# Two down projections: a second pair of weight pieces in seven products, and products with high weights first

## The reference, cut to what matters

```python
hn = rms_norm_2(h, norm_ffn_g)
gate, up = jnp.split(hn @ w_gate_up, 2, axis=-1)      # 2048 -> 2 x 5632
h = h + (jax.nn.silu(gate) * up) @ w_down             # 5632 -> 2048
out = rms_norm_2(h, norm_final_g)
```

## Time and profile before

| what | value |
|---|---|
| median of 3 runs | 2610.51 us |
| the profiled execution | 2610.58 us |
| its span, first to last instruction | 2608.8 us |
| TensorE multiplications | 2600.0 us busy, 21492 of them |
| VectorE busy | 1679.9 us (64%) |
| ScalarE busy | 1186.8 us (45%) |
| granted clock of TensorE in the span | 1.000 |

### The profile page before, as it was taken

The page is one execution under the profiler, slowest core; times in us unless marked ns, Lnnn a source line. Parts: engine busy times, 40 slices in busy tenths (PEclk is TensorE's granted clock), DMA queues, the critical chain, the costliest instruction groups (busy, mean ns, idle before and its releaser), DMA issues.

```text
span 2608.8 us, 50524 instructions
## 1 busy us (share of the span) xinstructions
PE 2600.0 (100%) x21492; PEld 2547.7 (98%) x21492; DVE 1679.9 (64%) x1795; ACT 1186.8 (45%) x1280; POOL 14.6 (1%) x33
## 2 busy tenths in 40 slices
PE   9999999999999999999999999999999999999998
PEld 8989999999999999999999999999999989998997
DVE  7668765555555556795676666556777775567566
ACT  5356544434443444465443433444544444444444
POOL 2000000000000000000000000000000000000000
PEclk9999999999999999999999999999999999999999
DMA  9654556555655565555555555655565556555653
GB/s 307 202 168 163 196 191 197 186 201 187 198 187 200 188 199 191 178 203 197 178 194 189 184 190 182 196 191 194 194 210 194 193 194 203 193 186 196 208 189 134
DMA packets 254460, 504.29 MB, mean 193 GB/s; under 512 B 9390, under 2 KB 11712, under 8 KB 254160
## 3 DMA queue, kind: packets, MB, share of 16 engines
q1 hardware_dynamic: 250160, 496.14, 57.2%
q10 hardware_dynamic: 3136, 4.34, 0.5%
q0 software_dynamic: 992, 1.34, 0.2%
HBM read 498.89 MB, written 2.89 MB: 192 GB/s over the span
## 4 chain that ended last, share of the span: by engine, by line
PE 100%; ACT 0%; DVE 0%; DVEq 0%; POOL 0%; issue 0%; POOLq 0%
PE ps L1608 49%; PE ps L1619 25%; PE ps L1686 4%; PE ps L1695 4%; PE ps L1690 3%; PE ps L1636 3%; PE ps L1638 3%; PE ps L1637 3%; PE ps L1810 1%; PE ps L1646 1%; PE ps L1647 1%; PE ps L1809 1%; PE ps L1808 1%; PE ps L1644 1%; PE ps L1654 0%; PE ps L1561 0%
## 5 line engine op out<-in xcount | busy, mean ns | idle before, releaser
L963 DVE TENSOR_TENSOR lo<-raw,hi 128x1024 fp32r<-128x1024 f32 x939 | 1139.8, 1224 | 799.0 <-ACT hi L597 786.1
L597 ACT ACTIVATE hi<-raw 128x1024 fp32r<-128x1024 f32 x939 | 989.9, 1060 | 1206.7 <-PE ps L1619 923.4
L1608 PE MATMUL ps<-A,hi 128*128 128x256 f32 x7286 | 902.8, 276 | 0.0
L1608 PEld LDWEIGHTS ps<-A,hi 128*128 128x128 f32 x7286 | 861.0, 188 | 0.3
L1608 PE MATMUL ps<-B,hi 128*128 128x256 f32 x3963 | 491.0, 276 | 0.0
L1619 PE MATMUL ps<-A,lo 128*128 128x256 f32 x3648 | 487.7, 276 | 0.0
L1608 PEld LDWEIGHTS ps<-B,hi 128*128 128x128 f32 x3963 | 468.2, 188 | 0.1
L1619 PEld LDWEIGHTS ps<-A,lo 128*128 128x128 f32 x3648 | 447.4, 188 | 0.0
L1619 PE MATMUL ps<-B,lo 128*128 128x256 f32 x1984 | 265.2, 276 | 0.0
L1619 PEld LDWEIGHTS ps<-B,lo 128*128 128x128 f32 x1984 | 243.3, 188 | 0.0
L1686 PE MATMUL ps<-B,hi 128*128 128x260 f32 (+3 forms) x768 | 109.1, 284 | 0.0
(11 more groups left out here) (311 smaller groups left out, 1524.2 us busy)
## 6 DMA issues: line engine op xcount, KB each, us to landing
raw<-in_w_in_dram SPq DMA_DIRECT2D x135, 1024.0 KB, 5.2
raw<-in_ffn_w_dram SPq DMA_DIRECT2D x132, 1024.0 KB, 5.1
raw<-in_w_gate_up_dram SPq DMA_DIRECT2D x88, 1024.0 KB, 5.1
raw<-in_w_down_dram SPq DMA_DIRECT2D x44, 1024.0 KB, 5.1
raw<-in_w_out_dram SPq DMA_DIRECT2D x16, 1024.0 KB, 5.1
raw<-in_pl_w_gate_dram SPq DMA_DIRECT2D x16, 1024.0 KB, 5.1
raw<-in_conv_out_w_dram SPq DMA_DIRECT2D x16, 1024.0 KB, 5.0
raw<-in_w_o_dram SPq DMA_DIRECT2D x16, 1024.0 KB, 5.1
```

Of the source, the lines that this page charges most:

```text
L597: act.activation(hi[:, slot % RING], raw[:, raw_slot, 2 * (slot % 2):2 * (slot % 2) + 2, :], ACT.Copy).then_inc(hi_ready, 1)
L963: dve.tensor_tensor(lo[:, slot % RING], raw[:, slot // 2 % RAWS, 2 * (slot % 2):2 * (slot % 2) + 2, :], hi[:, slot % RING], ALU.subtract). ...
L1608: pe.matmul(ps[:, b0 + m, 0:T], high(slot, kk, m), x, start=j == 0 and kk == 0 and part == 0, stop=False)
```

## The change

In three of the four groups of `f2_down0` and `f2_down1` a second pair (pieces 6 and 7) is done in seven products; the group (0,0) keeps one pair, and `f2_down2` its single one. The activation sums of the rows of these pieces are made behind the fourth up group. And in all three down projections the products with the high part of a weight piece come first, those with its low part behind a wait of their own, in plain pieces (`tokens_highs_first`), in pairs and in the pairs' block sums.

```diff
-PAIRS_AT = {"f2_down0": (2,), "f2_down1": (2,), "f2_down2": (2,)}
-SUMS_BEHIND = {"f2_up0": (1,), "f2_up1": (1,), "f2_up2": (1,)}
-PAIR_ROWS = range(4, 8)
+PAIRS_AT = {"f2_down0": (2, 6), "f2_down1": (2, 6), "f2_down2": (2,)}
+TWO_PAIRS_IN = ((0, 1), (1, 0), (1, 1))
+SUMS_BEHIND = {"f2_up0": (1, 3), "f2_up1": (1, 3), "f2_up2": (1,)}
+PAIR_ROWS = (*range(4, 8), *range(12, 16))
...
-    return [(x, x.p0 + turn * x.per_turn + g * x.pieces)
+    return [(x, x.p0 + turn * x.per_turn + g * x.pieces, PAIRS_AT[x.name] if (turn, g) in TWO_PAIRS_IN else PAIRS_AT[x.name][:1])
...
+            def tokens_highs_first(seg, j, slot, b0, n):
+
+                closes = j == seg.pieces - 1 or n + 1 in PAIRS and j == seg.pieces - 3 or n == TOTAL - RING - 1
+                pe.wait_ge(hi_ready, n + 1)
+                for kk in range(2):
+                    k = 2 * j + kk
+                    for a in range(2):
+                        for part in range(2):
+                            pe.matmul(ps[:, b0 + a, :], tokens_at(k)[part][:, k, a * P:(a + 1) * P], hi[:, slot % RING, kk, :],
+                                      start=j == 0 and kk == 0 and part == 0, stop=False)
+                pe.wait_ge(lo_ready, n + 1)
+                for kk in range(2):
+                    k = 2 * j + kk
+                    for a in range(2):
+                        last = pe.matmul(ps[:, b0 + a, :], tokens_at(k)[0][:, k, a * P:(a + 1) * P], lo[:, slot % RING, kk, :],
+                                         start=False, stop=closes and kk == 1)
+                last.then_inc(pieces_used, 1)
...
                 for i in range(2):
                     k = 2 * (j + i)
+                    pe.wait_ge(hi_ready, n + i + 1)
+                    by_high(p16[:, 0:half], u == 0 and i == 0, tokens(0, k), block(0, 0, i)[0])
+                    by_high(z0[:, 0:half], False, tokens(0, k + 1), block(1, 0, i)[0])
+                    by_high(z0[:, half:GC], False, summed(3, i), block(1, 1, i)[0])
+                    by_high(p57[:, 0:half], u == 0 and i == 0, summed(0, i), block(0, 1, i)[0])
                     pe.wait_ge(lo_ready, n + i + 1)
-                    product(p16[:, 0:half], u == 0 and i == 0, False, tokens(0, k), *block(0, 0, i))
...
+                    by_low(p16[:, 0:half], False, tokens(0, k), block(0, 0, i)[1])
...
+                pe.wait_ge(t_hi_ready, q + 1)
...
                             elif seg.reads[1] == "wide" or seg.reads[1] == "conv" and not two_passes(seg, g):
                                 with_meta(seg, g, j, slot, b0, n)
+                            elif seg.name.startswith("f2_down"):
+                                tokens_highs_first(seg, j, slot, b0, n)
```

More of the change, by code:

```diff
@@ L217, in seven_product_pairs @@
     pairs, groups = {}, {}
-    for i, (x, first) in enumerate(down_groups(segs)):
-        for u, j in enumerate(PAIRS_AT[x.name]):
+    for i, (x, first, places) in enumerate(down_groups(segs)):
+        for u, j in enumerate(places):
             pairs[first + j] = (len(pairs), sum(len(PAIRS_AT[f"f2_down{c}"]) for c in range(int(x.name[-1]))) + u, u)
@@ L1805, in seven_products, with by_high, by_low @@
                 last_pair = u == 1 or n + 4 not in PAIRS
[L1807 to L1810, removed]
+                def by_high(to, start, x, w):
+                    pe.matmul(to, x[0], w, start=start, stop=False, skip_group_check=True)
+                    pe.matmul(to, x[1], w, start=False, stop=False, skip_group_check=True)
+                def by_low(to, stop, x, w):
+                    return pe.matmul(to, x[0], w, start=False, stop=stop, skip_group_check=True)
                 def tokens(a, k):
@@ L1828, in seven_products @@
                     k = 2 * (j + i)
-                    pe.wait_ge(lo_ready, n + i + 1)
-                    product(p16[:, 0:half], u == 0 and i == 0, False, tokens(0, k), *block(0, 0, i))
-                    product(z0[:, 0:half], False, closes and i == 1, tokens(0, k + 1), *block(1, 0, i))
-                    product(z0[:, half:GC], False, closes and i == 1, summed(3, i), *block(1, 1, i))
-                    product(p57[:, 0:half], u == 0 and i == 0, False, summed(0, i), *block(0, 1, i)).then_inc(pieces_used, 1)
+                    pe.wait_ge(hi_ready, n + i + 1)
[3 more added lines that the diff above has]
+                    by_high(p57[:, 0:half], u == 0 and i == 0, summed(0, i), block(0, 1, i)[0])
+                    pe.wait_ge(lo_ready, n + i + 1)
+                    by_low(p16[:, 0:half], False, tokens(0, k), block(0, 0, i)[1])
+                    by_low(z0[:, 0:half], closes and i == 1, tokens(0, k + 1), block(1, 0, i)[1])
+                    by_low(z0[:, half:GC], closes and i == 1, summed(3, i), block(1, 1, i)[1])
+                    by_low(p57[:, 0:half], False, summed(0, i), block(0, 1, i)[1]).then_inc(pieces_used, 1)
+                pe.wait_ge(t_hi_ready, q + 1)
+                for i in range(2):
+                    k = 2 * (j + i)
+                    by_high(p16[:, half:GC], False, summed(1, i), block_sum(1, i)[0])
+                    by_high(p57[:, half:GC], False, summed(2, i), block_sum(0, i)[0])
+                    by_high(z1[:, 0:half], False, tokens(1, k + 1), block_sum(2, i)[0])
                 pe.wait_ge(t_lo_ready, q + 1)
@@ L1836, in seven_products @@
                     k = 2 * (j + i)
-                    product(p16[:, half:GC], False, last_pair and i == 1, summed(1, i), *block_sum(1, i))
-                    product(p57[:, half:GC], False, last_pair and i == 1, summed(2, i), *block_sum(0, i))
-                    last = product(z1[:, 0:half], False, closes and i == 1, tokens(1, k + 1), *block_sum(2, i))
+                    by_low(p16[:, half:GC], last_pair and i == 1, summed(1, i), block_sum(1, i)[1])
+                    by_low(p57[:, half:GC], last_pair and i == 1, summed(2, i), block_sum(0, i)[1])
+                    last = by_low(z1[:, 0:half], closes and i == 1, tokens(1, k + 1), block_sum(2, i)[1])
                 last.then_inc(t_used, 1)
```

## The result

The changed kernel takes 2620.34 us (median of 6 runs, 2620.10 to 2620.61), against 2610.51 of the kernel before: a ratio of 1.0038, 95% interval 1.0026 to 1.0049. It is slower, by 9.8 us, and lies outside the predicted range (2606.5 to 2611.2).

The account below looks back on a forecast made before the run. TensorE's multiplications were taken to bound the kernel, filling 2600.0 of 2608.8 us. Saved multiplications of 2.96 us, 0 for the new order and 0.76 us of waits gave -2.20 on 2610.58, so 2608.4 us, range 2606.5 to 2611.2.

Parts of the forecast that it names:

- Term 1: Down projections: six second pairs replace plain pieces, each saving 0.49 us of TensorE multiplications, 2.96 us less in all.
- Term 2: Down projections, high weights first: no multiplications added, spacing effect 0; pair's second low part used 0.94 us later.
- Term 3: Two-pair groups: VectorE needs 21.77 us against TensorE's 20.78, so TensorE waits 0.38 us per projection's fourth group, 0.76 in all.
- third rival: Plain pieces of down projections: splitting products sharing a stationary block costs loads, 0.0044 us per multiplication, 2611.2 us; chance 0.07.
- first rival: Down projections: TensorE never waits, 2607.6 us, or its short multiplications also come closer, 2607.1 us; chance 0.18.
- second rival: Hand-over inside a pair: VectorE loses time between its steps when ScalarE is late, up to 2616.8 us; chance 0.13.

Follow-up runs that it names:

- the order alone: The kernel before with high weights first in all down projections' plain pieces and pairs, still one pair per group: 2610.59 us (before: 2610.62).
- the second pairs alone: The kernel before with second pairs in three of four groups, products in the old order: 2624.71 us.
- the kernel with the cut of 128: The changed kernel with the split at the start of f2_up1 and f2_up2 at 128 and 128 columns, not 248 and 8: 2608.39 us, ratio 0.9992.

## Why the prediction was wrong, point by point

**Term 1 held.** A two-pair group is 21.27 - 20.79 = 0.48 us shorter than one with a single pair (0.49 forecast), and a pair takes 4.94 (4.95).

**Term 2 held where it looked.** The pairs keep 0.118, the plain pieces 0.227, and the new waits cost nothing; the order alone is worth 0.0 us. As a cover for VectorE's delay it was priced rightly too (the second pairs alone).

**Term 3 held.** VectorE takes 21.77 us for a two-pair group, as summed; the wait falls at the first pair of the fourth group and nowhere else, and makes that group 0.41 us longer for 0.38 forecast. The sum of the three terms, -2.20, was measured as -2.11 in the two projections, and as -2.17 in the kernel with the cut of 128. That this kernel took 2608.39 where 2608.4 was forecast is luck in the last digit: the terms were right to about 0.1.

**The step that failed** is the one in the first paragraph, on which the sum stands: that the time "moves only by what is taken out of them or by a wait that appears". It takes the spacing of every multiplication outside the change as given. The spacing of 2695 of them wasn't: +11.82 us, a term that the sum doesn't have. The prediction saw both spacings, 0.113 in the up projections and 0.118 in the pairs, and asked which of them the changed instructions would get. It did not ask what makes an up projection run at 0.113, though the trace of before showed it: at 2145.97 the first four of f2_up1 stand 0.12 apart, then comes the split, and then 0.113. The kernel's table asks for a split that has no use in the arithmetic. Such a line is a question to put to the trace, and it wasn't put. The third rival had the right size, 0.0044 us for each multiplication, at the wrong place: in 648 multiplications of the plain pieces, not in 2695 of the projections behind. The first rival (no wait, or a shorter spacing in the pairs) and the second (VectorE's hand-over) did not occur. The 0.04 given to a slower kernel was counted from the second rival's waits, so it had nothing to do with what came.

The edit to blame is the second pair in the last group of a projection: it puts a pair directly ahead of f2_up1 and f2_up2 where plain pieces of 512 columns stood. That is shown from both sides (the pairs alone bring the loss; the same number of pairs with a plain end don't). What stays open is why a split of 248 and 8 changes the spacing over behind plain pieces and not behind a pair, while 192 and 64 or 128 and 128 do in the changed kernel. The number of instructions, the length of the stretch, TensorE's wait in the fourth group (it is there with two second pairs too) and the granted clock are excluded; what in the pair it is (its addresses, the banks that it writes, the blocks that it loads) wasn't tried apart.

The traces hold a hint that no run tested. It is in TensorE's weight loads. The changed kernel from 2150 to 2300 us, and the same stretch with the cut of 128 (count, busy us, mean ns):

```profile
L1609 PEld LDWEIGHTS ps<-A,hi 128*128 128x128 f32 x845 | 103.7, 189 | 0.0
L1609 PEld LDWEIGHTS ps<-A,hi 128*128 128x128 f32 x877 | 103.8, 188 | 0.0
```

The difference of 1 ns in the mean is every third load. At the longer spacing it lasts 192 ns and the two others 187 or 188 (in f2_up1 of the kernel before without the split, 512 of 1536 loads); at the shorter one only one to three loads at a split do. In the six runs with a split of 248 and 8 that worked, one load of 187 or 188 ns lay between the last long one and the load of the first split multiplication, in both projections. In the changed kernel and with the pairs alone, at all 14 splits, the long load came directly ahead of it. So the end in a pair goes with a cycle of three that is shifted by one, and the split may fail for its place in this cycle. The two runs that moved the split couldn't tell, since they moved it by multiples of three; a move by one or two multiplications could. In the pairs themselves all loads last 186 to 190 ns, without such a cycle.

## What to carry to other kernels

Where one engine is busy all the time, check before the sum that the untouched stretches behind a change will run as before: compare the spacing at their start with the spacing later, and find what changed it. A line in a tuned kernel that does nothing for the result (a multiplication split in two, a dummy step) is a lever on the machine; if the change alters what stands directly ahead of it, price it at its full worth, here 11 us. And after a change, read stage lengths first: a change can deliver all that it was forecast to and lose it elsewhere.

## What the runs showed of the hardware

Multiplications of 256 columns with the clock granted at 1.00 (the 2.4 GHz level) in the gate and up projections had two spacings, 0.1133 and 0.1178 us, each of which lasted over a thousand multiplications and through whole turns. f2_up1 and f2_up2 began at the longer one in every run here, behind 512-column multiplications and behind a pair alike. They stayed there without a split (180.91 us for f2_up1) and went to the shorter one behind a split of 128 and 128 or 192 and 64 in each run that had it, and behind one of 248 and 8 where no pair stood directly ahead of the projection. The Trainium skill's page "TensorE: Matmul & The Clock Gate", section "Back-to-back issue gap", gives N / 2.4 GHz and 2.5 ns for a multiplication by itself, by estimate 109 ns for 256 columns, and says that in a stream with weight loads both set the spacing. The rows here show 113 and 118 ns for one and the same stream, and the measurement decides. A split costs 0.11 to 0.13 us. A turn of 384 multiplications at the shorter spacing is 1.7 us faster, and the spacing lasts from turn to turn, so one split at the start of a projection is enough.
